# Walking the sparse-attention steps from the widest query block to the narrowest

## The chip, the cores and the metric

One core of a Trainium2 chip runs the whole program. The metric is the device time of one execution in microseconds. The kernel before takes 3139.21 us, the median of 3 runs (3135.36 to 3140.19).

## The reference, cut to what matters

The program is one transformer layer with three mixers (compressed, selected and windowed attention; an mLSTM; attention to a memory), then two further layers of feed-forward, pooling and convolution blocks. The change touches the selected and the windowed attention alone. There are 512 tokens, 16 heads of 64 in 4 groups that share keys and values, and a head sees all earlier tokens in both branches, because the 16 blocks that may be selected are more than the 8 there are, and the window is as long as the sequence:

```python
s = jnp.einsum('bqghd,bkgd->bghqk', qi, ks) * NSA_SCALE
p = masked_softmax(s, mask).astype(vs.dtype)      # mask: key position <= query position
return jnp.einsum('bghqk,bkgd->bqghd', p, vs)
```

`y_nsa` is the gated sum of the three results, `gb[..., 0:1] * o_cmp + gb[..., 1:2] * o_slc + gb[..., 2:3] * o_win`.

## The kernel before, in words

Every engine has its own instruction stream, in order; semaphores tie them together. The attention is a loop over the 4 groups (`with pe.Fori(0, GROUPS) as g`, and its like on each engine). A pass starts with the query projection (24 rounds of three matmuls), goes on with the scores against the compressed keys (32 matmuls of 32 columns, L1360 and L1361 through `stacked`), and then walks 32 steps. A step is one (branch, query block, head): `STEPS` at L93 lists them, branch 0 selected and branch 1 windowed, four query blocks of 128 tokens, four heads. Query block qb sees keys up to its own end, so its step is qb + 1 key blocks wide: 128, 256, 384 or 512 columns. The text says a step of 1, 2, 3 or 4 blocks. The steps are numbered i = 0 to 31, and with the order before they are 1, 2, 3, 4, 1, 2, 3, 4 blocks wide, four steps of each.

A step i passes through this chain:

- TensorE, `scores(i)` at iteration i: two matmuls into bank 2 or 3 (i even or odd). It waits until mask step i - 2 has read that bank.
- VectorE, `mask_step(i)` at L1876: adds the causal mask, scales, takes the row extreme and writes `prob`.
- ScalarE, `exp_step(i)` at L872: the exponential in place, with row sums.
- TensorE, `turn(i)` at iteration i + 2 (L1385): one transpose for each key block, into bank 5 or 6.
- `turn_step(i)`: copies them to `probT`; ScalarE does the even steps (L880), VectorE the odd ones (L1884). Both issue it at iteration i + 2, after that iteration's exponential or mask.
- TensorE, `weigh(i)` at iteration i + 3 (L1395): two instructions of 64 columns for each key block.

TensorE's iteration i is thus `scores(i)`, `turn(i - 2)`, `weigh(i - 3)` and then three merge-gate matmuls of 512 columns (`gates(GATE_STEP)`, L1334), which are work for later that fills the steps:

```python
for i in range(NS + 3):
    if i < NS:
        scores(i)
    if 2 <= i < NS + 2:
        turn(i - 2)
    if i >= 3:
        weigh(i - 3)
    gates(GATE_STEP)
```

Other work stands at fixed iterations of the same streams, whatever step falls there. VectorE does pieces of the compressed attention after the masks 1, 2, 4, 5 and 6 (`between`; after mask 5 it is `cmp_mask`, L1856, a product of two operands in SBUF) and `out_step` (six small instructions, L1889 to L1899) at every fourth iteration from 8 to 36. ScalarE splits gate weights with `high_in_loop` (L654) after iterations 2, 16 and 32, and evacuates a gate tile with `gate_evac` (L890, then a store) at iterations 8, 16, 24 and 32; at 16 and 32 the two stand one behind the other. GpSimd makes the low part (L1068) as soon as ScalarE's high part is there. Behind the steps come the transposes of the compressed probabilities (L1411), twelve gate matmuls, their 32 products (L1418), the remaining gates and the transposes of the result (L1425).

Of the kernel before, what the change touches and what calls it, by code (L numbers as in the profile page):

```python
# [17 lines left out]
TT = T // P  # L18
# [8 lines left out]
GROUPS, HPG, DH = 4, 4, 64  # L27
# [62 lines left out]
N_UNITS = U_FFN[4] + PER_FFN  # L90


STEPS = [(br, qb, hh) for br in range(2) for qb in range(TT) for hh in range(HPG)]  # L93
NS = len(STEPS)
S_BANK = (2, 3)
OUT_BANK = (7, 1)
# [113 lines left out]
def build(nc, A, const_in, invcount_in, out):  # L210
    with ExitStack() as ctx:
# [435 lines left out]
        def _(act):  # L647
# [213 lines left out]
            with act.Fori(0, GROUPS) as g:  # L861
# [6 lines left out]
                def exp_step(i):  # L868
                    br, qb, hh = STEPS[i]
                    n = P * (qb + 1)  # L870
                    act.wait_ge(s_m, g * NS + (i + 1))
                    nc.scalar.activation(prob[i % 4][:, 0:n], prob[i % 4][:, 0:n], ACT.Exp, bias=nmax[:, i:i + 1], scale=-1.0,  # L872
                                         accum_out=psum_row[:, i:i + 1]).then_inc(s_e, 1)

                def turn_step(i):
                    if i % 2 == 0:
                        br, qb, hh = STEPS[i]
                        n = P * (qb + 1)
# [222 lines left out]
        def _(pe):  # L1101
# [219 lines left out]
            with pe.Fori(0, GROUPS) as g:  # L1321
# [50 lines left out]
                def scores(i):  # L1372
                    br, qb, hh = STEPS[i]
                    n = P * (qb + 1)
                    if i >= len(S_BANK):
                        pe.wait_ge(s_m, g * NS + (i + 1 - len(S_BANK)))
                    stacked(bank[S_BANK[i % len(S_BANK)]][:, 0:n], hh, qb, [k_st[br][0][:, 0:n], k_st[br][1][:, 0:n]]).then_inc(s_s, 1)

                def turn(i):
                    br, qb, hh = STEPS[i]  # L1380
                    pe.wait_ge(s_e, g * NS + (i + 1))
                    if i >= 2:
                        pe.wait_ge(s_pa if i % 2 == 0 else s_pd, g * (NS // 2) + i // 2)
                    for kb in range(qb + 1):
                        ins = nc.tensor.transpose(bank[5 + i % 2][:, kb * P:(kb + 1) * P], prob[i % 4][:, kb * P:(kb + 1) * P], ident)  # L1385
                    ins.then_inc(s_t, 1)

                def weigh(i):
                    br, qb, hh = STEPS[i]
                    pe.wait_ge(s_pa if i % 2 == 0 else s_pd, g * (NS // 2) + (i // 2 + 1))  # L1390
                    if i % HPG == 0 and i >= 2 * HPG:
                        pe.wait_ge(s_or, g * (NS // HPG) + (i // HPG - 1))
                    c = DH * hh
                    for kb in range(qb + 1):
                        ins = nc.tensor.matmul(bank[OUT_BANK[i // HPG % 2]][:, c:c + DH], probT[i % 4][:, kb * P:(kb + 1) * P],  # L1395
                                               v_sw[br][:, kb, bass.ds(g * DH, DH)], start=kb == 0, stop=kb == qb)
                    ins.then_inc(s_o, 1)
# [827 lines left out]
```

## Time and profile before

| | before |
|---|---|
| median of 3 runs | 3139.21 us |
| the profiled execution | 3136.1 us, its span 3134.3 us |
| granted TensorE clock, mean | 0.962 |
| TensorE busy | 2910.9 us (93%), 13386 matmuls |
| VectorE, ScalarE, GpSimd busy | 1513.3, 887.5, 341.1 us |
| the attention loop | about 384 to 790 us of the span |

The span is what lies between the first and the last instruction; 1.8 us lie around it. A matmul counts as busy for as long as it is in the array, and its neighbours overlap with it, so what a stretch of TensorE costs is read from start to start. The granted clock is 1.00 at 2.4 GHz and 0.50 at 1.2 GHz; a value between is a mean over a stretch with both.

### The profile page before, as it was taken

The page shows a single profiled execution, that of the slowest core. Times are in us where ns is not written, and L with a number is a line of the kernel's source. Part 1 is how long each engine was busy: PE and PEld are TensorE (multiplying, and loading weights), DVE is VectorE, ACT ScalarE, POOL GpSimd, SP SyncE. Part 2 cuts the span into 40 slices and gives each one's busy share as a digit, 9 for nine tenths or more (in the row PEclk, how much of TensorE's full clock was granted, in tenths as well). Part 3 has the DMA queues.
Part 4 walks back from the last instruction along what each step waited for, and adds up shares of the span by engine and source line. Part 5 has one row for each costly group of instructions (what it writes and reads, how often), then busy time and mean ns, then how long its engine had stood idle before and what let it go on. Part 6 is the DMA issues. An engine that isn't in the chain of part 4 may idle for free.

```text
span 3134.3 us, 34634 instructions
## 1 busy us (share of the span) xinstructions
PE 2910.9 (93%) x13386; PEld 2382.4 (76%) x13386; DVE 1513.3 (48%) x2168; ACT 887.5 (28%) x1206; POOL 341.1 (11%) x70
## 2 busy tenths in 40 slices
PE   6998799999898999899997699999999889899997
PEld 6777688888776888778885588887888765578886
DVE  2334354445457443464534845444543379555532
ACT  4333343334233222222221322122222232332211
POOL 4222111111310000000000000000000056100000
PEclk9998899899999999999998899999999999999999
DMA  6221112221441232323222122332232221122232
GB/s 193 85 67 61 54 43 83 67 71 44 144 154 54 94 106 87 101 68 106 94 93 82 51 97 94 101 101 81 94 104 91 88 68 41 55 80 94 94 98 71
DMA packets 255085, 270.43 MB, mean 86 GB/s; under 512 B 5695, under 2 KB 243407, under 8 KB 254858
## 3 DMA queue, kind: packets, MB, share of 16 engines
q1 hardware_dynamic: 250688, 261.77, 26.1%
q10 hardware_dynamic: 4298, 7.36, 0.6%
q8 instruction: 60, 0.98, 0.1%
q14 instruction: 39, 0.32, 0.0%
HBM read 258.62 MB, written 10.49 MB: 86 GB/s over the span
## 4 chain that ended last, share of the span: by engine, by line
PE 69%; issue 16%; DVE 6%; POOL 5%; ACT 2%; DMA 1%; SPq 0%; POOLq 0%; DVEq 0%; ACTq 0%
PE bank L1114 20%; PE bank L1115 20%; PE bank L1116 20%; POOL w_lo L1074 3%; POOL w_lo L1068 3%; PE bank L1566 1%; PE bank L1129 1%; PE bank L1131 1%; PE bank L1130 1%; DVE rstd L1989 1%; ACT w_hi L662 1%; PE bank L1142 1%; PE bank L1144 0%; PE bank L1143 0%; DVE w_lo L1954 0%
## 5 line engine op out<-in xcount | busy, mean ns | idle before, releaser
L1114 PE MATMUL bank<-h_hi,w_hi 128*128 128x512 f32 x2064 | 817.5, 396 | 53.5 <-POOL w_lo L1074 25.1
L1115 PE MATMUL bank<-h_lo,w_hi 128*128 128x512 f32 x2064 | 811.3, 393 | 0.0
L1116 PE MATMUL bank<-h_hi,w_lo 128*128 128x512 f32 x2064 | 810.6, 393 | 0.0
L1954 DVE TENSOR_TENSOR w_lo<-w_raw,w_hi 128x2048 fp32r<-128x2048 f32 (+2 forms) x176 | 390.3, 2220 | 391.7 <-ACT w_hi L662 325.7
L1114 PEld LDWEIGHTS bank<-h_hi,w_hi 128*128 128x128 f32 x2064 | 392.6, 190 | 144.5 <-POOL w_lo L1074 29.3
L1116 PEld LDWEIGHTS bank<-h_hi,w_lo 128*128 128x128 f32 x2064 | 392.5, 190 | 83.1
L1115 PEld LDWEIGHTS bank<-h_lo,w_hi 128*128 128x128 f32 x2064 | 392.9, 190 | 82.5 <-issue 1.2
L1114 PE MATMUL bank<-hid_hi,w_hi 128*128 128x512 f32 x880 | 343.5, 390 | 0.0
L1116 PE MATMUL bank<-hid_hi,w_lo 128*128 128x512 f32 x880 | 342.4, 389 | 0.0
L1115 PE MATMUL bank<-hid_lo,w_hi 128*128 128x512 f32 x880 | 342.4, 389 | 0.0
L654 ACT ACTIVATE w_hi<-w_raw 128x2048 fp32r<-128x2048 f32 x124 | 237.0, 1911 | 356.7 <-PE bank L1116 349.3
L1074 POOL TENSOR_TENSOR w_lo<-w_raw,w_hi 128x2048 fp32r<-128x2048 f32 x34 | 217.8, 6410 | 1097.6 <-ACT w_hi L662 1097.6
L662 ACT ACTIVATE w_hi<-w_raw 128x2048 fp32r<-128x2048 f32 (+2 forms) x110 | 199.5, 1818 | 409.2 <-PE bank L1116 401.5
L955 ACT ACTIVATE gate_tmp<-gate_tmp 128x512 f32<-128x512 f32 x110 | 67.7, 633 | 483.8 <-DVE gate_tmp L2036 483.8
L2044 DVE TENSOR_TENSOR gate_tmp<-gate_tmp,bank 128x512 f32<-128x512 f32 x110 | 75.6, 687 | 254.1 <-PE bank L1116 252.1
L1115 PEld LDWEIGHTS bank<-hid_lo,w_hi 128*128 128x128 f32 x880 | 165.2, 188 | 35.0 <-issue 0.7
L1114 PEld LDWEIGHTS bank<-hid_hi,w_hi 128*128 128x128 f32 x880 | 165.2, 188 | 35.0 <-issue 0.7
L1116 PEld LDWEIGHTS bank<-hid_hi,w_lo 128*128 128x128 f32 x880 | 165.2, 188 | 34.3
L2036 DVE TENSOR_TENSOR gate_tmp<-bank,rstd 128x512 f32<-128x512 f32 x110 | 70.9, 686 | 183.4 <-PE bank L1116 183.3
L1068 POOL TENSOR_TENSOR w_lo<-w_raw,w_hi 128x2048 fp32r<-128x2048 f32 x24 | 110.1, 4590 | 448.4 <-ACT w_hi L654 448.4
L872 ACT ACTIVATE prob<-prob,nsa_stat 128x128 f32<-128x128 f32 (+3 forms) x128 | 72.1, 563 | 158.4 <-DVE nsa_stat L1876 157.5
L1876 DVE CUSTOM_DVE_ANT_0 prob<-bank,const_masks 128x128 f32<-128x128 f32 (+3 forms) x128 | 62.8, 491 | 106.3 <-PE bank L1361 73.3
(355 smaller groups left out, 3489.1 us busy)
## 6 DMA issues: line engine op xcount, KB each, us to landing
w_raw<-in_ffn_w_in_dram SPq DMA_DIRECT2D x88, 1024.0 KB, 5.1
w_raw<-in_w_in_dram SPq DMA_DIRECT2D x32, 1024.0 KB, 5.4
w_raw<-in_ffn_w_out_dram SPq DMA_DIRECT2D x32, 1024.0 KB, 5.1
w_raw<-in_w_ffn_in_dram SPq DMA_DIRECT2D x22, 1024.0 KB, 5.1
w_raw<-in_ffn_w_out_dram SPq DMA_DIRECT2D x16, 768.0 KB, 4.5
w_raw<-in_conv_w_pw_dram SPq DMA_DIRECT2D x12, 1024.0 KB, 5.5
w_raw<-in_w_ffn_down_dram SPq DMA_DIRECT2D x8, 1024.0 KB, 5.1
gate_scratch<-gate_stage ACTq DMA_DIRECT2D x24, 256.0 KB, 2.0
```

What stands on the lines that cost most here:

```text
L654: nc.scalar.activation(w_hi[slot][:, :], raw[s][:, :], ACT.Copy).then_inc(w_hi_ready, 1)
L662: nc.scalar.activation(w_hi[SLOT[u]][:, 0:n], raw[s][:, 0:n], ACT.Copy).then_inc(w_hi_ready, 1)
L872: nc.scalar.activation(prob[i % 4][:, 0:n], prob[i % 4][:, 0:n], ACT.Exp, bias=nmax[:, i:i + 1], scale=-1.0, accum_out=psum_row[:, i:i + 1 ...
L955: nc.scalar.activation(tg[t][:, :], tg[t][:, :], ACT.Silu).then_inc(silu_done, 1)
L1068: nc.gpsimd.tensor_tensor(w_lo[s][:, :], raw[s][:, :], w_hi[s][:, :].bitcast(F32), ALU.subtract).then_inc(w_lo_ready, 1)
L1074: nc.gpsimd.tensor_tensor(w_lo[d][:, :], raw[u % 2][:, :], w_hi[d][:, :].bitcast(F32), ALU.subtract).then_inc(w_lo_ready, 1)
L1114: nc.tensor.matmul(bank[b][:, 0:n], wh, xh, start=first, stop=False)
L1115: nc.tensor.matmul(bank[b][:, 0:n], wh, xl, start=False, stop=False)
L1116: ins = nc.tensor.matmul(bank[b][:, 0:n], wl, xh, start=False, stop=last)
L1954: v.tensor_tensor(w_lo[slot][:, 0:n], raw[s][:, 0:n], w_hi[slot][:, 0:n].bitcast(F32), ALU.subtract).then_inc(w_lo_ready, 1)
L2036: v.tensor_tensor(tg[t][:, :], bank[b + t][:, :], rb[:, :], ALU.mult).then_inc(g_scaled, 1)
L2044: mark(v.tensor_tensor(tg[t][:, :], tg[t][:, :], bank[b + 2 + t][:, :], ALU.mult), up_read, n + (t + 1))
```

## The change

The query blocks are walked from the last to the first in both branches. The steps are then 4, 3, 2, 1, 4, 3, 2, 1 blocks wide. All else stays: the instructions, their shapes and counts, the iterations at which the other work stands, buffers, banks and semaphores.

```diff
-STEPS = [(br, qb, hh) for br in range(2) for qb in range(TT) for hh in range(HPG)]
+STEPS = [(br, qb, hh) for br in range(2) for qb in reversed(range(TT)) for hh in range(HPG)]
```

## Rows read from the trace of the kernel before

**Rows 1.** Page, part 4: the chain that ended last, by engine.
```profile
PE 69%; issue 16%; DVE 6%; POOL 5%; ACT 2%; DMA 1%; SPq 0%; POOLq 0%; DVEq 0%; ACTq 0%
```
**Rows 2.** Windows, steps of pass 1: busy by engine (instructions), clock, DMA share, GB/s.
```profile
497.50:565.20 67.70, 64.71 (x412) 56.55 (x412) 36.94 (x132) 34.14 (x88) 10.37 (x3) 0.97 0.14 47
```
**Rows 3.** Waits of TensorE, 384 to 800 us: total, times, longest.
```profile
PE bank L1395 <- DVE probT L1884: 8.8, 4, 2.2
PE bank L1395 <- ACT probT L880: 2.4, 6, 0.5
```
**Rows 4.** Timeline, TensorE, pass 1: start, duration, instruction, [idle before <- releaser].
```profile
502.69 0.43 PE L1395 MATMUL bank<-v_sel,probT 128*128 x2 [0.22 <-ACT probT L880]
...
505.94 0.43 PE L1395 MATMUL bank<-v_sel,probT 128*128 x2 [0.46 <-ACT probT L880]
...
509.76 0.43 PE L1395 MATMUL bank<-v_sel,probT 128*128 x2 [2.18 <-DVE probT L1884]
```
**Rows 5.** Timeline, VectorE, pass 1, iteration 5.
```profile
506.59 2.92 DVE L1856 TENSOR_TENSOR p_cmp<-p_cmp,const_masks 128x496 f32<-128x496 f32 x1
509.43 0.28 DVE L1884 COPY probT<-bank 128x128 f32<-128x128 f32 x1
```
**Rows 6.** Timeline, ScalarE and GpSimd, pass 1, behind iteration 2.
```profile
502.44 1.91 ACT L654 ACTIVATE w_hi<-w_raw 128x2048 fp32r<-128x2048 f32 x1
...
504.43 4.55 POOL L1068 TENSOR_TENSOR w_lo<-w_raw,w_hi 128x2048 fp32r<-128x2048 f32 x1 [18.56 <-ACT w_hi L654]
```
**Rows 7.** Windows behind that wait, in passes 0, 2 and 3.
```profile
405.50:412.40 6.90, 6.09 (x22) 5.42 (x22) 2.38 (x10) 1.47 (x5) 0.02 (x1) 0.52 0.49 152
...
610.40:617.30 6.90, 5.81 (x20) 5.14 (x21) 2.48 (x9) 1.47 (x5) 0.30 (x1) 0.51 0.50 152
...
716.20:719.70 3.50, 3.50 (x16) 3.11 (x15) 1.00 (x4) 0.60 (x2) 0.00 (x0) 0.52 0.70 246
```
**Rows 8.** Timeline, TensorE: weigh(3) and weigh(11) of pass 0, weigh(11) of pass 1.
```profile
406.31 0.69 PE L1395 MATMUL bank<-v_sel,probT 128*128 x2 [2.19 <-DVE probT L1884]
...
424.49 0.78 PE L1395 MATMUL bank<-v_sel,probT 128*128 x6
...
525.21 0.78 PE L1395 MATMUL bank<-v_sel,probT 128*128 x6
```
**Rows 9.** Timeline, TensorE: the next weigh, one wide iteration later.
```profile
527.49 1.00 PE L1395 MATMUL bank<-v_sel,probT 128*128 x8
```
**Rows 10.** Timeline, TensorE, a narrow iteration: turn(17), weigh(16), first gate, next scores.
```profile
535.58 0.30 PE L1385 MATMUL bank<-identity_ones,prob 128*128 128x128 f32 x1
535.72 0.33 PE L1395 MATMUL bank<-v_win,probT 128*128 x2
535.86 0.48 PE L1334 MATMUL bank<-h_hi,w_hi 128*128 128x512 f32 x1
...
536.63 0.28 PE L1360 MATMUL bank<-k_win_high_twice,q_stacked 128*128 128x256 f32 x1
```
**Rows 11.** Timeline, pass 1, step 12 (4 blocks): scores, mask, exponential, then copy(10).
```profile
520.01 0.39 PE L1360 MATMUL bank<-k_sel_high_twice,q_stacked 128*128 128x512 f32 x1
...
520.85 0.69 DVE L1876 CUSTOM_DVE_ANT_0 prob<-bank,const_masks 128x512 f32<-128x512 f32 x1 [1.28 <-PE bank L1361]
...
521.58 0.73 ACT L872 ACTIVATE prob<-prob,nsa_stat 128x512 f32<-128x512 f32 x1 [1.74 <-DVE nsa_stat L1876]
...
522.30 0.47 ACT L880 ACTIVATE probT<-bank 128x384 f32<-128x384 f32 x1
```
**Rows 12.** Timeline, ScalarE, pass 1, iteration 16: gate evacuation, then weight split.
```profile
530.84 0.58 ACT L890 ACTIVATE gate_stage<-bank 128x512 f32<-128x512 f32 x1
...
532.04 1.92 ACT L654 ACTIVATE w_hi<-w_raw 128x2048 fp32r<-128x2048 f32 x1 [0.61 <-ACT gate_stage L890]
```
**Rows 13.** Timeline, TensorE, pass 1, iteration 21: turn(19), then weigh(18).
```profile
538.12 0.27 PE L1385 MATMUL bank<-identity_ones,prob 128*128 128x128 f32 x1
538.53 0.43 PE L1395 MATMUL bank<-v_win,probT 128*128 x2
```

## The prediction

> **What bounds the kernel now.** I read the page's chain first: TensorE is 69% of it and no other engine above 6% [rows 1], so the change pays only where TensorE stands still or runs slow. The change acts in the steps of the attention loop alone. In pass 1 they take 67.7 us, from the first wide scores to the transposes behind them, and TensorE is busy for 64.71 of them at a clock of 0.97; VectorE is busy for 36.9 and ScalarE for 34.1 [rows 2]. No engine beside TensorE is near its limit; what can be won or lost is the 3 us or so of waits. Then the waits of TensorE over the four passes: 8.8 us in four waits for VectorE's `probT` copy and 2.4 us in six for ScalarE's, all at `weigh` [rows 3]. The timeline of pass 1 puts them in the first six iterations: weigh(0) 0.22, weigh(2) 0.46, weigh(3) 2.18 us [rows 4], 2.86 in all. Two things lie behind the last one. ScalarE splits gate weights for 1.91 us after iteration 2, and GpSimd then works for 4.55 us, until 508.98. VectorE's `cmp_mask` falls into that time: it takes 2.92 us and ends when GpSimd ends, and copy(3) starts behind it, 0.45 us after GpSimd's end [rows 5, 6]. Last, the granted clock: behind that same wait it went to 1.2 GHz for 6.9, 6.9 and 3.5 us in passes 0, 2 and 3 [rows 7], and not in pass 1 [rows 2]. Pass 0 needs 18.18 us from weigh(3) to weigh(11), pass 1 15.45 [rows 4, 8]: the slow stretch of 6.9 us costs 2.73, or 0.40 us for each us of it. The three stretches, 17.3 us, cost 6.8 us. These are the places at which the order can act.
>
> **What the change leaves alone.** Counts and shapes are the same, so TensorE's own work is the same and only its order differs. SP's queue has no instruction tied to a step's width; ScalarE's gate stores and GpSimd's splits keep their iterations, and move in time by a few us with them. The key loads of a pass end ahead of step 0 in both orders. I cost all this at nothing; what hides it is that the split weights of a gate are used some eight iterations after they are made, 10 us or more in either order.
>
> **Prices.** A wide iteration takes 527.49 - 525.21 = 2.28 us between two weighs [rows 8, 9]. A narrow one (one block) is turn 0.14, weigh 0.14, gates 0.77 [rows 10]; with its scores (0.17 by estimate) 1.2 us. For four blocks I take scores 0.46 [rows 11], turn 0.43 and weigh 0.80, by estimate from the wide iteration less its scores and gates. The latencies of step 12 are: scores to mask 0.84, mask to exponential 0.73, exponential to the next instruction of ScalarE 0.72 [rows 11]. A one-block copy takes 0.28, and weigh starts 0.05 after it [rows 4, 5]; a four-block copy is 0.58, by estimate from 0.28 and the 0.47 of three blocks [rows 5, 11]. A gate evacuation holds ScalarE for 1.20 us, a weight split for 1.92 [rows 12].
>
> **Part 1, the start of a pass (steps 0 to 3 go from one block to four).** I follow pass 1 from 497.50 with the new widths. TensorE needs about 2.0 us an iteration while the clock is still low there, then 1.7 to 2.5. Iteration 2 begins at 501.5 and iteration 3 at 503.2. ScalarE's exponential 2 runs 503.1 to 503.8, copy(0) is ready at 504.4, and TensorE comes for it at 504.05: a wait of 0.4. The weight split starts at 504.3, so GpSimd works from 506.3 to 510.8, 1.9 us later than before. The masks slide further: iteration 5 begins at 508.4, mask 5 ends at 509.6 and `cmp_mask` is held from there, to 511.3 instead of 509.4. Copy(3), now four blocks, is ready at 512.0, and TensorE, busy with wider work until then, comes for it at 511.45: a wait of 0.55 in place of 2.18. In all 0.9 us for 2.86 in pass 1; over four passes 3.6 for the 11.2 of [rows 3], **-7.6 us**. Bounds: -11.2 if TensorE never waits, 0 if `cmp_mask` is held as long as before.
>
> **Part 2, the slow clock behind it.** With a longest wait of 0.55 us at this place I expect no fall of the clock, and the 6.8 us come back: **-6.8 us**. Bounds: 0, and -6.8. The rule that speaks against this is in the Trainium skill, "TensorE: Matmul & The Clock Gate", section "HAM oscillation — how this bites in real kernels": its rule of thumb lets a kernel lose the clock only by idle gaps longer than any here. By that rule the slow stretches have another cause and the 6.8 us stay lost; it is a rival below. The trace has the stretches behind this wait in three passes of four, and I go by that.
>
> **Part 3, the jump from step 15 to step 16.** Before, the widths fell from four to one here, where ScalarE does an evacuation and a split one behind the other; after, they rise from one to four, and TensorE carries one-block turns and weighs over the latencies of four-block steps. Let scores(16) start at 0. Mask 0.84, exponential 1.57, copy(14) 2.29, ready 2.62. TensorE comes for it after 0.46 + 0.14 + 0.14 + 0.77 (iteration 16) and 0.46 + 0.14: at 2.11. Wait **0.51**. Iteration 18 then starts at 3.53 and takes 1.80 with turn(16); iteration 19 starts at 5.33 and wants turn(17) at 5.79. ScalarE evacuates from 2.46, splits from 3.66 to 5.58, and only then does exponential 17 (queued behind it), so turn(17) may start about 0.87 later, at 6.45: wait **0.66**. Exponential 18 starts at 6.3, copy(16) at 7.0, ready at 7.65, and TensorE comes at 6.88: wait **0.77**. Behind it, copy(17) on VectorE is in time. The sum is 1.94 us a pass, 7.8 in four. Before, the only wait at this place is the 0.41 from turn(19) to weigh(18), where 0.14 is the work [rows 10, 13]: 0.27 a pass, 1.1 in four. The difference is **+6.7 us**. Bounds: 0 if ScalarE's split were through in time, and twice the sum, +14.5, if each link is late by as much again.
>
> **Part 4, the other places.** Where widths fall (4 to 3, 3 to 2, 2 to 1) the work in flight is wider than the latency to be covered. Among one-block steps TensorE comes for an even copy 0.1 us after it is ready, by the same sums; two such runs a pass, between 0 and +1.5 us in all; I take 0. At the end of a pass the drain after step 31 is narrow: ScalarE's split of iteration 32 still ends 1 us before the transposes L1411 do. VectorE's copy(31) stands behind an `out_step` and is 0.35 us early. Price 0; if that cover were gone, up to 0.5 us a pass.
>
> **Sum.** -7.6 - 6.8 + 6.7 = **-7.7 us** against the profiled execution's 3136.1 us: 3128.4. The median of the runs is 3.1 us above the profiled one; with the same offset the time is **3131.5 us**, 0.25% less.
>
> **The rivals.**
> - *The clock falls at the new jump as it fell at the old wait.* The three new waits lie within 5 us. For: three passes of four fell behind 2.2 us of waiting. Against: the single waits are a third of it and wide work stands between them. The gain of part 2 is then taken back: -7.7 + 6.8 = -0.9, 3138.3 us. The rule on idle gaps cited above leads to the same time another way: the slow stretches stay where they are.
> - *Slower: ScalarE's queue at iteration 16.* Exponentials 17 and 18 and copy(16) stand behind evacuation and split, and TensorE has only narrow work in flight. If the waits are twice what I compute (+7.8) and each pass then loses the clock for 6.9 us (4 x 2.73 = +10.9), the change gives -7.7 + 7.8 + 10.9 = +11.0, 3150 us. It decides from about 2 us of waiting close together; I compute 1.4 for the two that are neighbours.
> - *Faster still: the jump is hidden.* If copy(14) and the split come in time, part 3 is -1.1 instead of +6.7, and the sum is -15.5: 3124 us. Against it is the plain order of ScalarE's queue.
> - *Nothing moves.* The trace has no room for the order to be without effect on weigh(3); that the gains and losses cancel is covered by the first rival.
>
> **How the numbers follow.** Forecast 0.46, first rival 0.27, slower rival 0.10, hidden jump 0.12, anything else 0.05. This kernel's measurement can tell a difference of about 0.2%, 6.3 us, from no change, so faster means below 3132.9. The forecast lies 1.4 us on the fast side of that; with a spread of some 4 us in its own terms I count 0.30 of it as faster and 0.16 as the same. With the hidden jump and a part of the first rival, faster is 0.48; same is 0.40, most of it the first rival; slower is 0.12. The range runs from the hidden jump with part 4 as it is, less 1 us for what the clock may give, 3123, to the first rival with the upper bound of part 4 and 3 us of spread between executions, 3143. About 2 in 10 is left out.
>
> **What the profile would show.** Right: weigh(3)'s wait below 1 us in each pass and `cmp_mask` below 2.9 us; clock 1.0 from iteration 6 to 15; new waits at weigh(14), turn(17) and weigh(16), 0.5 to 0.8 us each, the latter two released by ScalarE; nothing new at the end of a pass. Wrong: waits at the jump with the clock at 0.5 behind them; the wait at weigh(3) as long as before; or copy(31) and the split of iteration 32 late at the end of a pass.

## The result and the profile after

The changed kernel takes **3121.78 us** (median of 6 runs, 3111.47 to 3124.37). The kernel before, run beside it and earlier, takes 3137.55 us (median of 6, 3128.11 to 3140.56). The ratio is 0.9947, with a 95% interval of 0.9933 to 0.9960: 15.8 us less, where 7.7 were forecast. The sign was right, the time lies 1.2 us below the range.

| | before | after |
|---|---|---|
| median | 3137.55 us | 3121.78 us |
| the profiled execution, its span | 3136.1, 3134.3 us | 3124.37, 3122.5 us |
| mean granted clock | 0.962 | 0.963 |
| steps of passes 0, 1, 2, 3 | 70.8, 67.7, 70.0, 69.2 us | 66.7, 66.2, 65.9, 65.9 us |
| TensorE's waits at the probT copies | 11.2 us in 10 | 7.5 us in 16 |

The page's chain is the one of [rows 1], to the digit:

```profile
PE 69%; issue 16%; DVE 6%; POOL 5%; ACT 2%; DMA 1%; SPq 0%; POOLq 0%; DVEq 0%; ACTq 0%
```

The steps of the four passes, as windows (span; busy time of TensorE, its weight loads, VectorE, ScalarE and GpSimd with counts; clock; DMA share; GB/s). The second line answers [rows 2]:

```profile
395.60:462.30 66.70, 64.67 (x411) 56.78 (x412) 34.96 (x133) 33.32 (x88) 9.15 (x2) 0.96 0.15 48
496.20:562.40 66.20, 63.94 (x411) 56.33 (x412) 35.01 (x133) 33.33 (x88) 9.13 (x2) 0.97 0.15 48
595.20:661.10 65.90, 63.77 (x411) 56.17 (x411) 34.89 (x132) 33.23 (x88) 9.13 (x2) 0.97 0.15 48
694.10:760.00 65.90, 63.83 (x412) 56.23 (x412) 34.96 (x133) 33.30 (x88) 9.14 (x2) 0.97 0.14 48
```

The passes took 277.7 us before (first wide scores to the transposes, by the starts of the instructions) and take 264.6 now: 13.1 us less. All four are alike now, at a clock of 0.96 or 0.97; before, only pass 1 had 0.97. The time at 1.2 GHz within the steps, summed over the passes, fell from 32.5 to 15.7 us. The whole profiled execution is 11.8 us shorter. Most of the difference lies ahead of the loop, which the change does not touch: pass 0 comes to its first scores at 395.59 instead of 393.68, 1.9 us later, with a mean clock of 0.92 in the first 384 us instead of 0.93. The two profiled executions also lie differently among their runs: before's is 1.5 us below its median, after's 2.6 above.

TensorE's waits from 384 to 800 us, which answer [rows 3], and the timeline of pass 1 at the start (TensorE, VectorE, GpSimd), which answers [rows 4] to [rows 6]:

```profile
PE bank L1395 <- ACT probT L880: 6.6, 12, 0.7
...
PE bank L1385 <- ACT prob L872: 1.0, 4, 0.3
PE bank L1395 <- DVE probT L1884: 0.9, 4, 0.3
```

```profile
503.62 1.10 PE L1395 MATMUL bank<-v_sel,probT 128*128 x8 [0.68 <-ACT probT L880]
...
505.35 4.58 POOL L1068 TENSOR_TENSOR w_lo<-w_raw,w_hi 128x2048 fp32r<-128x2048 f32 x1 [22.60 <-ACT w_hi L654]
...
508.88 1.59 DVE L1856 TENSOR_TENSOR p_cmp<-p_cmp,const_masks 128x496 f32<-128x496 f32 x1
510.39 0.68 DVE L1884 COPY probT<-bank 128x512 f32<-128x512 f32 x1
...
511.12 1.10 PE L1395 MATMUL bank<-v_sel,probT 128*128 x8 [0.25 <-DVE probT L1884]
```

The wait at weigh(3) is 0.25 us instead of 2.18. `cmp_mask` still runs into GpSimd's split (it ends 0.5 us behind it, as before), but it arrives later in it: 1.59 us instead of 2.92. The clock behind the wait, which answers [rows 7], is 1.00 in each of the four passes:

```profile
409.00:416.00 7.00, 6.79 (x49) 6.09 (x49) 4.34 (x12) 2.60 (x8) 0.84 (x1) 1.00 0.49 152
509.00:516.00 7.00, 6.75 (x49) 6.07 (x48) 4.44 (x12) 2.56 (x8) 0.94 (x1) 1.00 0.48 150
608.00:615.00 7.00, 6.80 (x48) 6.10 (x48) 4.30 (x13) 2.60 (x8) 0.71 (x1) 1.00 0.49 150
707.00:714.00 7.00, 6.78 (x47) 6.05 (x47) 4.26 (x14) 2.57 (x9) 0.56 (x1) 1.00 0.44 150
```

And the jump from step 15 to step 16 in pass 1. The lines are turn(15) and weigh(14), ScalarE's split, then turn(17) and weigh(16); the places answer [rows 12] and [rows 13]:

```profile
529.88 0.27 PE L1385 MATMUL bank<-identity_ones,prob 128*128 128x128 f32 x1
530.52 0.43 PE L1395 MATMUL bank<-v_sel,probT 128*128 x2 [0.38 <-ACT probT L880]
...
531.57 1.92 ACT L654 ACTIVATE w_hi<-w_raw 128x2048 fp32r<-128x2048 f32 x1 [0.61 <-ACT gate_stage L890]
533.39 0.70 ACT L872 ACTIVATE prob<-prob,nsa_stat 128x512 f32<-128x512 f32 x1
...
534.24 0.66 PE L1385 MATMUL bank<-identity_ones,prob 128*128 128x128 f32 x4 [0.25 <-ACT prob L872]
535.60 1.07 PE L1395 MATMUL bank<-v_win,probT 128*128 x8 [0.70 <-ACT probT L880]
```

The three waits are there, at the instructions that were named. The idle time that the view gives is a little less than the delay, because a matmul's modelled end reaches into it. From start to start, less the price of the work, weigh(14) is 0.51 us late (0.64 from turn(15), 0.13 of it work), turn(17) 0.40 and weigh(16) 0.93: 1.84 us a pass, where 1.94 were worked out.

### The profile page after: what moved, and what is told of

It reads as the page before. It is cut to its first block, busy times and chain, and to the rows that moved or that the text cites. A ratio compares the mean times of both kernels' runs of the same rounds, so it can differ in the third digit from the quotient of the medians.

```text
span 3122.5 us, 34634 instructions
## 1 busy us (share of the span) xinstructions
PE 2900.4 (93%) x13386; PEld 2375.3 (76%) x13386; DVE 1494.5 (48%) x2168; ACT 886.2 (28%) x1206; POOL 340.9 (11%) x70
## 4 chain that ended last, share of the span: by engine, by line
PE 69%; issue 16%; DVE 6%; POOL 5%; ACT 2%; DMA 1%; SPq 0%; POOLq 0%; DVEq 0%; ACTq 0%
PE bank L1114 20%; PE bank L1115 20%; PE bank L1116 20%; POOL w_lo L1074 3%; POOL w_lo L1068 3%; PE bank L1566 1%; PE bank L1129 1%; PE bank L1131 1%; PE bank L1130 1%; DVE rstd L1989 1%; ACT w_hi L662 1%; PE bank L1142 1%; PE bank L1144 0%; PE bank L1143 0%; DVE w_lo L1954 0%
## 5 line engine op out<-in xcount | busy, mean ns | idle before, releaser
L955 ACT ACTIVATE gate_tmp<-gate_tmp 128x512 f32<-128x512 f32 x110 | 67.7, 632 | 483.9 <-DVE gate_tmp L2036 483.9
L1876 DVE CUSTOM_DVE_ANT_0 prob<-bank,const_masks 128x512 f32<-128x512 f32 (+3 forms) x128 | 62.8, 491 | 113.4 <-PE bank L1361 72.4
L872 ACT ACTIVATE prob<-prob,nsa_stat 128x512 f32<-128x512 f32 (+3 forms) x128 | 71.8, 561 | 157.7 <-DVE nsa_stat L1876 157.6
```

What stands on the lines that cost most here:

```text
L955: nc.scalar.activation(tg[t][:, :], tg[t][:, :], ACT.Silu).then_inc(silu_done, 1)
```

## The experiments

Every kernel below does the whole computation. Differences under about 4 us are within what the intervals allow, so I give the ratio to the kernel before, which ran beside each on the same chip. Beside it I give how long the steps of the four passes take together in the profiled execution (277.7 us before, 264.6 after), read as above. It is one execution of each kernel, but stretches at full clock repeat from pass to pass to about 0.1 us, and what happens outside the steps does not enter.

**The collision alone, in the order of before.**

```diff
-between = {1: cmp_max, 2: cmp_shift, 4: cmp_sum, 5: cmp_mask, 6: cmp_gain}
+between = {1: cmp_max, 2: cmp_shift, 4: cmp_sum, 9: cmp_mask, 10: cmp_gain}
```

> The order of before; only cmp_mask and the piece behind it go from iterations 5 and 6 to 9 and 10, when GpSimd is through with its split. Theory (the collision with GpSimd makes the 2.2 us wait, and the wait makes the clock fall): cmp_mask takes 0.7 us, weigh(3) does not wait, no slow stretch behind it; -8.8 us and -6.8 us, about 3122 us. Rival (narrow steps leave TensorE too little work, whatever VectorE does): weigh(3) still waits over 1 us and the gain is below 3 us. Rival on the clock: the waits go but the slow stretches stay, -8.8 us, 3129 us.

Measured: 3120.57 us, ratio 0.9948 (0.9935 to 0.9962), 15.7 us less than the kernel before beside it (3136.31). `cmp_mask` takes 0.67 us, its steps take 262.4 us, 15.3 less than before (15.6 were forecast), no wait for VectorE's copy is left in the view, and the clock is 1.00 behind its old place in all four passes:

```profile
510.11 0.67 DVE L1856 TENSOR_TENSOR p_cmp<-p_cmp,const_masks 128x496 f32<-128x496 f32 x1
```

```profile
402.00:416.00 14.00, 13.51 (x85) 11.54 (x84) 7.62 (x29) 7.16 (x22) 4.24 (x1) 1.00 0.29 95
501.00:515.00 14.00, 13.52 (x85) 11.54 (x84) 7.96 (x30) 7.83 (x25) 4.58 (x1) 1.00 0.29 94
...
699.00:713.00 14.00, 13.52 (x86) 11.59 (x85) 7.96 (x30) 8.25 (x25) 4.59 (x1) 1.00 0.27 94
```

With the steps still from narrow to wide, moving `cmp_mask` and the piece behind it by four iterations gives as much as the change does. So the long wait and the slow stretches behind it come from the collision, not from too little work for TensorE in narrow steps. That the two medians agree to 0.1 us is luck: in the changed kernel the waits of the jump and the gains of part 4, which this experiment does not have, nearly cancel.

**Both removals at once.** The same edit on the changed kernel.

> The changed kernel, and also cmp_mask and the piece behind it at iterations 9 and 10. Theory (reversing the order and moving cmp_mask remove the same wait and the same slow stretch): only the 0.2 us a pass that weigh(3) still waits are left to win, -0.9 us against the changed kernel, 3121 us. Rival (the two gains are of different kinds and add up): some 12 us more, 3109 us.

Measured: 3121.72 us, ratio 0.9960 (0.9945 to 0.9975). The steps take 263.0 us, 1.6 less than in the changed kernel, of which 0.9 is the wait at weigh(3). The rival would have been 12 us faster. The reversal and the late `cmp_mask` remove the same wait, and the second to come finds almost nothing left.

**One branch reversed.** These two undo half of the change each. The cuts (`...`) leave out what is the same:

```diff
-STEPS = [... for qb in reversed(range(TT)) ...]
+STEPS = [... for qb in (reversed(range(TT)) if br == 0 else range(TT)) ...]
```

> Widths 4, 3, 2, 1 and then 1, 2, 3, 4: only branch 0 is reversed. The start of a pass is that of the changed kernel; at iteration 16 the width does not rise, but TensorE has only one-block work in flight while ScalarE evacuates and splits. Theory (thin work over ScalarE's queue is what costs): waits at turn(17) of about 1.3 us and at weigh(16) of about 0.4, 1.7 a pass instead of 1.35, and the small gaps of rising widths are back in branch 1; some 3.5 us slower than the changed kernel, about 3125 us, 12 us under before. Rival (the rise from one to four blocks is what costs): the waits of 1.35 us a pass are gone, 5.4 us faster than the changed kernel, 3116 us.

Measured: 3126.8 us, ratio 0.9969 (0.9957 to 0.9981), 9.5 us under before; 3125 and 12 were expected. Against the changed kernel the 0.26 us at turn(17) have become 0.8; weigh(16) waits 0.38, and a wait of 0.48 for VectorE stands at weigh(19) in three passes of four. In pass 1:

```profile
531.28 0.33 PE L1385 MATMUL bank<-identity_ones,prob 128*128 128x128 f32 x1 [0.82 <-ACT prob L872]
531.99 0.41 PE L1395 MATMUL bank<-v_win,probT 128*128 x2 [0.38 <-ACT probT L880]
537.00 0.43 PE L1395 MATMUL bank<-v_win,probT 128*128 x2 [0.48 <-DVE probT L1884]
```

No width rises at iteration 16 here, and turn(17) and weigh(16) still wait, 1.2 us together where the changed kernel has 0.96 (its 0.38 at weigh(14) is gone, the 0.48 at weigh(19) is new). 1.7 were forecast for the two places. So what costs is that TensorE has only one-block work in flight while ScalarE evacuates and splits. The steps take 271.1 us, 6.5 more than in the changed kernel; 5.0 us more of them are at 1.2 GHz, 2.0 us by the 0.40 of the prediction. The clock fell behind these waits in one pass of four (0.56 from 733.4 to 737.0 us):

```profile
733.40:737.00 3.60, 3.55 (x13) 3.10 (x14) 1.03 (x5) 0.90 (x5) 3.46 (x1) 0.56 0.01 2
```

The mirror image reverses branch 1 only, `(range(TT) if br == 0 else reversed(range(TT)))`:

> Widths 1, 2, 3, 4 and then 4, 3, 2, 1: only branch 1 is reversed. The start of a pass is that of the kernel before: weigh(3) waits 2.2 us in each pass and the clock falls behind it in most. Theory: at iteration 16 wide work is in flight and no wait is left there (-1.1 us), and the small gaps of rising widths in branch 1 go (-1.5 us): about 3135 us, 2.6 us under before. Rival (the gain is spread over all steps, half of it in each branch): 8 us under before, 3130 us.

Measured: 3135.73 us, ratio 0.9995 (0.9986 to 1.0004), 0.6 us under before where 2.6 were expected; not distinguishable from no change. The start is that of before, with 8.8 us in four waits at weigh(3), and the clock fell behind all four of them, not three. No wait is left at iteration 16. So the part of the gain that the medians show belongs to branch 0, where the collision is. Branch 1 is not without effect, though: the steps take 274.3 us, 3.4 less than before, with as much time at 1.2 GHz in them (32.6 and 32.5 us). That is a little more than the 2.6 us forecast; the median does not show it, since behind the steps the clock was down for longer than before.

```profile
PE bank L1395 <- DVE probT L1884: 8.8, 4, 2.2
...
405.00:412.00 7.00, 6.13 (x22) 5.45 (x22) 2.48 (x10) 1.47 (x5) 0.09 (x1) 0.53 0.47 150
```

**The jump: the split moved.** In the changed kernel, ScalarE's stream:

```diff
-if GATE_EVAC[i] == 1:          # inside "if i in GATE_EVAC", i = 16
-    high_in_loop(g * 2 + (U_NSA // 2 + 1), 1, 1)
+if i == 20:
+    high_in_loop(g * 2 + (U_NSA // 2 + 1), 1, 1)
```

> The changed kernel with ScalarE's weight split moved from iteration 16 to iteration 20, where four-block weighs are in flight; the gate evacuation stays at 16. Theory (exponentials 17 and 18 and copy(16) stand behind the split): the waits at turn(17), 0.27, and weigh(16), 0.70, go, the one at weigh(14), 0.38, stays; -3.9 us against the changed kernel, about 3118 us. Rival (latency of the four-block steps makes these waits): no difference, or the wait is met again at iteration 20 to 22, 3121.8 us.

Measured: 3120.66 us, ratio 0.9948 (0.9935 to 0.9962). The waits moved as the theory says: turn(17)'s is gone, weigh(16)'s fell from 0.70 to 0.21 to 0.25, weigh(14)'s 0.38 stayed, and the sum of the waits at copies and turns fell from 8.5 to 5.4 us. The steps take 260.6 us, 4.0 less than in the changed kernel, with the same time at 1.2 GHz, as the theory has it. The median moved by 1.1 us only. In the profiled execution the rest was lost behind the steps, 3.2 us in the three stretches between the passes: in passes 0 to 2 the clock fell for 6.8 us some 3 us after the first of the 32 small products, where the changed kernel has no fall there in pass 0 and 3.4 us in the others. Here behind pass 0 and pass 1, this kernel first (mean 0.90 between the passes' steps), then the changed kernel (0.95):

```profile
460.20:493.70 33.50, 32.44 (x169) 27.61 (x167) 11.18 (x32) 8.22 (x11) 9.15 (x2) 0.90 0.36 111
559.50:593.00 33.50, 32.44 (x169) 27.61 (x167) 11.15 (x32) 8.20 (x11) 9.16 (x2) 0.90 0.36 111
```

```profile
462.30:496.20 33.90, 31.78 (x176) 27.29 (x175) 11.12 (x32) 8.16 (x11) 9.16 (x2) 0.95 0.36 110
562.40:595.20 32.80, 31.74 (x177) 26.83 (x175) 11.12 (x32) 8.16 (x11) 9.16 (x2) 0.95 0.36 113
```

The mechanism and its price are shown in the steps, and not in the time of the whole kernel. Whether the longer slow stretches come from the edit or by chance is open: nothing in that stretch was changed, only its place in time.

**ScalarE's copies ahead of its exponentials**, in the changed kernel:

```diff
 for i in range(NS + 2):
+    if i >= 2:
+        turn_step(i - 2)
     if i < NS:
         exp_step(i)
     ...
-    if i >= 2:
-        turn_step(i - 2)
```

> The changed kernel with ScalarE's copy(i-2) issued ahead of exponential i instead of behind it. Theory (weigh(0), weigh(14) and weigh(16) wait because the copy stands behind an exponential of four blocks): the waits at weigh(0), 0.5 to 0.7, and weigh(14), 0.38, go, weigh(16)'s shrinks to about 0.2, turn(17)'s 0.26 stays: -5 us against the changed kernel, 3117 us. Rival (the exponentials become late by as much as the copies become early): turn waits appear instead and the time stays at 3121 to 3123 us.

Measured: 3119.01 us, ratio 0.9954 (0.9938 to 0.9969). The waits for ScalarE's copies (6.6 us) are gone. In their place turn(17) waits 0.7 us for its exponential in each pass, 3.0 us in all instead of 1.0, and copies of VectorE 1.8 instead of 0.9. The steps take 260.5 us, 4.1 less than in the changed kernel where 5 were forecast, although 3.7 us more of them are at 1.2 GHz. The median moved by 2.8 us against the changed kernel, between the two expectations.

**The best of the above.** Widths 1, 2, 3, 4, 4, 3, 2, 1 with `cmp_mask` late, then the same with the copies first.

> Widths 1, 2, 3, 4, 4, 3, 2, 1 and cmp_mask at iteration 9. Theory: neither the wait behind cmp_mask nor one at iteration 16, and no small gaps of rising widths in branch 1: against the order of before with cmp_mask late (3120.6) -1.1 for the wait at weigh(18) and -2.7 for the small gaps, 3117 us. Rival (with the long wait gone the order of the steps is worth nothing): 3120 to 3121 us.

Measured: 3116.18 us, ratio 0.9944 (0.9928 to 0.9960), 18.7 us under the kernel before beside it (3134.92). Its own waits at the copies are 2.8 us. The steps take 258.5 us, 3.9 less than in the order of before with `cmp_mask` late (262.4); 3.8 were forecast.

> The same with ScalarE's copies ahead of its exponentials. Theory: the waits at weigh(0) and weigh(2), 0.3 and 0.46 us a pass, and the small gaps at even steps go too: -4 us against the kernel without that edit, 3113 us, and the fastest so far. Rival (exponentials late instead): the same time as without it, 3117 us.

Measured: 3114.40 us, ratio 0.9940 (0.9924 to 0.9955), 20.5 us under before: the fastest median of all, though its interval overlaps those of the changed kernel and of the one without the edit. One wait of 0.3 us at a copy is left in the loop. The steps take 254.9 us, 3.6 less than without the edit where 4 were forecast, although 5.8 us more of them are at 1.2 GHz; the medians are 1.8 us apart. The exponentials are not late in a way that costs: in the falling branch 1 the time from weigh(16) to weigh(31) is the same with the edit as without it (25.8 us), and in the rising branch 0 it is shorter with it, by an amount that matters below.

The steps of the four passes in the profiled executions, in us:

| kernel | steps | of them at 1.2 GHz |
|---|---|---|
| before | 277.7 | 32.5 |
| before, `cmp_mask` late | 262.4 | 15.3 |
| branch 1 reversed | 274.3 | 32.6 |
| branch 1 reversed, `cmp_mask` late | 258.5 | 15.4 |
| the same, copies first | 254.9 | 21.2 |
| branch 0 reversed | 271.1 | 20.7 |
| the changed kernel | 264.6 | 15.7 |
| changed, `cmp_mask` late | 263.0 | 15.2 |
| changed, split at 20 | 260.6 | 15.4 |
| changed, copies first | 260.5 | 19.4 |

## Why the prediction was wrong in size

| step of the prediction | forecast | measured in the profiles |
|---|---|---|
| part 1, waits at the start of a pass | -7.6 us | 11.2 to 3.15: -8.1 us |
| part 2, slow clock behind them | -6.8 us | no slow stretch left there: -6.8 us, by the same price |
| part 3, the jump at iteration 16 | +6.7 us | 1.84 x 4, less the 1.1 of before: +6.3 us |
| part 4, the other places | 0 | -3.9 us, worked out below |
| sum | -7.7 us | -12.5 us; the steps got 13.1 us shorter |

**Part 1** held, with its mechanism: the weight split later by the wider exponential and copy, `cmp_mask` held for less (1.59 us instead of 2.92, 1.7 worked out), and a wait of a quarter of a microsecond where 0.55 was worked out. GpSimd starts 9.1 us behind the pass's first wide scores instead of 6.9: 2.2 us later, for the 1.9 of the prediction. weigh(0) waits 0.47 to 0.68, where 0.4 was.

**Part 2** held. The experiment that removes only the collision keeps every other wait and has no slow stretch at the place; the one that keeps it has four. Over all runs: the two kernels with the long wait lost the clock behind it in seven passes of eight, the eight kernels without it in none of 32. The time at 1.2 GHz in the steps fell by 16.8 us, 6.7 by the 0.40 of the prediction. The rival that leaned on the Trainium skill ("TensorE: Matmul & The Clock Gate", section "HAM oscillation — how this bites in real kernels"), that gaps so short leave the clock alone, is refuted for this kernel by these counts.

**Part 3** held in its places, its releasers and its sum, to a tenth of a microsecond a pass. The single waits were further off: 0.51, 0.40 and 0.93 us for 0.51, 0.66 and 0.77, so the closeness of the sum is in part luck.

**Part 4 is the step that failed.** It put the other places at nothing, and they gave about 4 us. I priced the other places by asking only where the *new* order could lose, and took the old order's losses from the view of waits. That view lists only the larger ones. In the order before, every rise of a width (one to two blocks, two to three, three to four) put an even step's copy behind a wider exponential, and a weigh was late by 0.05 to 0.1 us, again and again. (One gap of each pass is of another kind: weigh(19), late by 0.2 us by the same prices, waits for VectorE's copy, which stands behind an `out_step`; there GpSimd was at its split, and the product at L1890 took 0.71 us instead of 0.17.) What that adds up to is seen from weigh(3) to weigh(15), and from weigh(16) to weigh(31), in pass 1 of both kernels, at full clock (weigh(3) is in [rows 4] and above, weigh(16) in [rows 10] and above). Before:

```profile
533.82 1.00 PE L1395 MATMUL bank<-v_sel,probT 128*128 x8
...
563.61 1.00 PE L1395 MATMUL bank<-v_win,probT 128*128 x8
```

After:

```profile
532.45 0.33 PE L1395 MATMUL bank<-v_sel,probT 128*128 x2
...
561.44 0.33 PE L1395 MATMUL bank<-v_win,probT 128*128 x2
```

The first stretch took 24.06 us and takes 21.33, of which 0.51 is the new wait at weigh(14): 3.24 us less without it. By the prices of the pieces (turn, weigh and scores of one to four blocks, read as in the prediction) the new order has 2.94 us less work between these two marks; 0.30 us is gaps. The second took 27.89 and takes 25.84. 1.10 us of that is work that lies on the other side of the marks, 0.27 the wait at weigh(18); 0.68 us is gaps. Together 0.98 us a pass, 3.9 us in four. That sum rests on my prices for the work on either side of the marks.

Two pairs of experiments show the same gaps without such prices. Branch 0: the best two kernels have the same order and differ only in whether ScalarE's copies stand behind its exponentials. From weigh(3) to weigh(15), with widths rising, the one without the edit takes 25.38 us in pass 1 and the one with it 24.81, and no wait stands between the marks in the view of either; over the four passes the difference is 2.1 us. Without the edit, then with it:

```profile
501.82 0.33 PE L1395 MATMUL bank<-v_sel,probT 128*128 x2
...
527.20 1.00 PE L1395 MATMUL bank<-v_sel,probT 128*128 x8
```

```profile
499.58 0.33 PE L1395 MATMUL bank<-v_sel,probT 128*128 x2
...
524.39 1.00 PE L1395 MATMUL bank<-v_sel,probT 128*128 x8
```

Branch 1: with `cmp_mask` late in both, reversing branch 1 makes the steps 3.9 us shorter (262.4 to 258.5), at the same time at 1.2 GHz and with the same work between the marks; 1.1 us of it is the wait at weigh(18), 2.8 is gaps, where 0.68 a pass was worked out. So the cause in branch 0, the copy behind the exponential, is shown by taking it away, and the size in branch 1 is measured. In branch 0 of the kernel before the gaps are less than 2.1 us, 1.2 by my prices: the copies behind the late weigh(3) probably gain a lead on TensorE while it waits, since the stretch from there takes 24.06 us, and 24.23 where only `cmp_mask` is late. That is argued, not shown.

**The offset and the range.** I carried the 3.1 us between the profiled execution and the median of three runs over to the changed kernel. With six runs that offset is 1.5 us for before, and after has one of the other sign, -2.6. That makes the remaining 4 us between the 11.8 of the profiles and the 15.8 of the medians. Of the 9.7 us by which the time was missed, the steps are 5.4, the rest of the execution takes 1.3 back, and this offset is 5.7, the larger part. With part 4 at -3.9 and the offset kept, the forecast would have been 3127.6 us, inside the range. The lower end of the range, 3123, was the hidden-jump case less 1 us; 3 us of spread between executions was given to the upper end only. With it at both ends, the time would have been inside.

**The chances.** The first rival (the clock falls at the new jump, 3138.3 us) and the slower one did not come about: the clock stayed at 1.00 behind the jump in all four passes. They were not empty: where only branch 0 was reversed, turn(17) waited 0.8 us and the clock fell behind these waits in one pass. That rival had too much weight, 0.27; the waits there were as worked out, the largest a third of the one that had brought the clock down.

## What to carry to other kernels

When a reordering wins, look for the one collision that it moved before crediting the order: here one 0.7 us instruction, held for 2.9 us while GpSimd worked, stood ahead of a copy that TensorE needed, and moving it, with the piece behind it, gave 15.7 us by itself. Price an idle wait of TensorE with the slow clock that follows it; here that nearly doubled it. And read the small gaps of the old order from start to start over a long stretch: a view of waits leaves out those that are each too short for it, and they were close to a third of the gain in the steps. When the median hardly moves, compare the stretch that the edit touches: here edits of 4 us showed there in full and in the medians in part.

## What the runs showed of the hardware that was not expected

- The clock may also fall behind waits far shorter than the 2.2 us that I watched: with branch 0 alone reversed, waits of 0.8 and 0.4 us close together had 3.6 us at 0.56 behind them in one pass of four. One pass does not show that the waits were the cause.
- `cmp_mask` took 0.67 us by itself, 1.59 and 2.92 us where it ran into GpSimd's 4.6 us split, and in both cases it ended 0.5 us behind GpSimd's end.
- The slow stretches behind the 32 small products differ between passes and kernels that issue the same instructions there (mean clock 0.90 or 0.95 over the same 33 us). A gain of 4.0 us in the steps was masked by them to 1.1 us in the median.
